# Operand sums spread over the tiles, S3 weights in their own buffer, and a new order of loads, scans and attention around the Strassen products of a hybrid decoder block

## The chip, the cores and the metric

The kernel runs on one core of one Trainium2 chip. The metric is device time in microseconds (us) of one execution, lower is better. The profile was taken in one execution of its own.

## The reference

One decoder block for 2048 tokens of width 1024 in float32, cut here to what matters:

```python
h = rms_norm(x, norm_g)
proj = h @ w_in                              # 1024 x 8704: the largest product
u_ssm, z_ssm, q, k, v, z_attn, q_mem, z_mem, gate_logits = split(proj)
y = gelu(s5_ssm(u_ssm, ...))                 # 48 groups of 16 channels, state 64
y = y * sigmoid(y @ w_glu + b_glu)
o_ssm = y * silu(z_ssm)
o_attn = dilated_window_attention(q, k, v) * silu(z_attn)    # 12 heads of 64, 3 dilations
o_mem = softmax(q_mem @ k_mem.T) @ v_mem * silu(z_mem)       # 4 heads, 256 keys from mem
gates = sigmoid(gate_logits + b_gate)
merged = gates[0] * (o_ssm @ w_br_ssm) + gates[1] * (o_attn @ w_br_attn) + gates[2] * (o_mem @ w_br_mem)
out = rms_norm(x + merged @ w_out, final_norm_g)
```

## The kernel before

**Split products.** Every float32 product is made of three matmuls. Each operand is split into a high part, rounded for the matmul, and a low part, the rest: `three_pass` (line 137) issues high·high (line 138), high·low (139) and low·high (140). The high part comes from a copy on ScalarE (ACT), the low part from a subtraction on VectorE (DVE).

**Stages.** From 0 to about 92 us the kernel normalises x, makes the keys and values of `mem` and the first two tiles of the projection. To about 698 us follow the projection's tiles n = 2 to 27, each 128 columns of `w_in` for all 2048 tokens, in four chunks c of 512 tokens. ACT copies a chunk out of its bank (line 1425), GpSimd (POOL) stores the tile (`store_tile`). Beside them DVE and ACT make the tables of the S5 scan in 12 units u of two tiles each, from n = 4 (`table_slot`; `combine`, line 1908, is one of their steps on DVE, `cs` on ACT at 1503 the cosines), whose small matrices PE multiplies at line 2703. SP stores them (`keep_inputs`, `keep_cosines`).

**The products of Strassen's form (Winograd's variant).** The other 40 tiles of the projection are done in 40 blocks b, each two tiles by half of the tokens (NBK = 40), with seven products instead of eight: A11, S2, S4, A12, S3, A22, S1 in that order, where the S4 of a block comes at step 2 of the next one. The S factors are sums of weights: S1 = A21 + A22 (`sum_s1`, line 2239), S3 = A11 − A21, S2 = S1 − A11, S4 = A12 − S2, each on DVE; then `factor_hi` on ACT and `factor_lo` on DVE (2263) split a factor into one of five places. S3 is written over A21, S2 over A11. SP loads the raw weights (`load_a11` and so on, line 1012). The other side are sums of h, the operands, made during the tiles by POOL: `make_operands(q)` makes the seven sums for one of 8 parts q in eight instructions (first line 1187) in the buffer `hx` and stores them; the next part waits for that store. Parts 0 to 3 belong to the first half of the tokens used, 4 to 7 to the second. The operands are loaded at the entry (line 1038), and exchanged for those of the other half of the tokens after blocks 7 and 27 (`SWAPS`): SP loads 1 MB per operand, `operand_hi` on ACT and `operand_lo` on DVE (2269) split it. DVE adds the products of a block up (`add_u2` 2281, `add_u3` 2288, `add_c12`, `add_c22` 2306); ACT finishes blocks (`finish`, 1463).

**The order beside the products.** Each engine runs the same loop over steps v = 7·row + at, with its own work of a step written out by hand, and all queues are in order. A block has eight side slots j (j = 8b to 8b + 7; s = j // 2), in which other work lies: the S5 scans in 24 pairs of groups (pair p at s = 4 + 2p; matmul 2725), then the bias tables, dilated attention in 40 batches (beat = j − 128 before the change; end at beat A_END = 102; matmuls 2809), attention into `mem` from M0 = A_END + 4 (queries at 2851), its weighing from C_FIRST, then the loads of y, GELU and the first split of y for the GLU product. From about 1794 us to 1893 runs the GLU product, then the branches' projections, the merge, the output projection and the norm.

Of the kernel before, what the change touches and what calls it, by code (L numbers as in the profile page):

```python
# [30 lines left out]
P = 128  # L31
# [31 lines left out]
def build_program(nc, x_t, mem_t, x_n, mem_n, norm_g, mem_norm_g, final_g, w_in, w_kv, b_gate, ssm_par, ssm_d, w_glu, b_glu,  # L63
                  w_br, w_out, rel_bias, buckets, ident_c, anti_c, sign_c, steps_c, powers_c, y_out):
    ctx = ExitStack()
    with ctx:
# [145 lines left out]
        def numbered(table, before=()):  # L212

            n = {x: k + 1 for k, x in enumerate(before)}
            for v in range(N_STEPS + NPR):
                row, at = divmod(v, NPR)
                for what, later in table.get(at, ()):
                    if 0 <= row + later < NBK:
# [6 lines left out]
                         5: ((A22, 1),), 6: ((S2, 1),)}, ((A11, 0), (A22, 0), (S2, 0)))  # L225
        SUM = numbered({4: ((S1, 1), (S3, 1)), 5: ((S2, 1),), 6: ((S4, 1),)},
# [74 lines left out]
        S0, S_BIAS = 4, 8  # L301
        grp_loaded = [sem(f"grp_loaded{i}") for i in range(R)]
# [49 lines left out]
        M0 = A_END + 4  # L352
# [6 lines left out]
        C_EXP, C_FIRST, N_WEIGH = M0 + 8, M0 + 20, NH // 2 * NQ  # L359
# [184 lines left out]
        w_s1, w_s4 = (keep1[:, k, :].rearrange("p (k m) -> p k m", k=4) for k in range(2))  # L544
        FACTOR_RAW = (w_a11, w_a11, w_s4, w_a12, w_a21, w_a22, w_s1)
# [4 lines left out]

        def product_bank(b, i):
            return bank(b, ("c11", "u", "c22", "c11", "u", "c21", "c22")[i])
# [37 lines left out]
        N_FIRST = len(FIRST)  # L590
        WARM = (22, 6)
# [117 lines left out]
        with nc.Block() as block:  # L709
            @block.sync  # L710
            def _(sp):
# [79 lines left out]
                def table_slot(n, c):  # L791
# [9 lines left out]
                    if 0 <= u - 1 < NU and w == 1:  # L801
                        keep_inputs(u - 1)
                        keep_cosines(u - 1, 1)
# [130 lines left out]
                def memory_beat(beat):  # L934
                    if beat == M0 - 1:
                        sp.wait_ge(o_mm, NT_B)
                        for i in range(2):
                            sp.wait_ge(stored[i], 16 * (N_Z // 2))
                            load_queries(i)
                        sp.wait_ge(st_mm, 1)  # L940
                        sp.wait_ge(o_raw, 16 * (NH // 2))
# [7 lines left out]
                        sp.wait_ge(st_out, 1)  # L949
                        for w in range(2):  # L950
                            sp.dma_start(st_d[w, 0:P, :], ptr[:, w, 0:P]).then_inc(st_kept, 16)
                            sp.dma_start(st_d[w, P:NH * NBLK, :], ptr[0:NH * NBLK - P, w, P:2 * P]).then_inc(
                                st_kept, 16)
                        load_stats()
# [17 lines left out]
                def attention_over():  # L972
                    for i in range(2):
                        sp.wait_ge(om_kept[i], 16 * MH)
                    for i in range(RW):
                        sp.wait_ge(oa_kept[i], 16 * N_WEIGH // RW)
# [2204 lines left out]
```

## Time and profile before

| what | value |
|---|---|
| time, median of 3 runs | 2433.62 us (2430.3 to 2434.28) |
| the profiled execution: its own time | 2435.78 us |
| the profiled execution: its span | 2434.0 us |
| mean granted TensorE clock | 0.992 of full speed |
| TensorE (PE) busy | 2351.8 us, 97% |
| VectorE (DVE) busy | 1812.0 us, 74% |
| ScalarE (ACT) busy | 790.5 us, 32% |
| GpSimd (POOL) busy | 288.9 us, 12% |

The span runs from the first to the last instruction that the profiler records; an execution's own time is somewhat longer. Busy times are sums of an engine's instructions. A wait is idle time of an engine, put down to the instruction or transfer that released it last. The granted clock is the share of full speed that TensorE had in a stretch.

### The profile page before, as it was taken

The numbers are of one execution on the slowest core, as the hardware profiler recorded it, in microseconds if no ns is written. First come the engines' busy times: TensorE is split into PE (matmuls) and PEld (weight loads), VectorE is DVE, ScalarE is ACT, GpSimd is POOL, SyncE is SP. The second block draws the span as 40 slices with busy tenths as digits, with TensorE's granted clock in tenths as the row PEclk, the third lists the DMA queues.
The fourth block names the chain that finished last, engine by engine and source line by source line (L and its number), as shares of the span: only waits on it lengthen the run. The fifth ranks groups of instructions, "written<-read, shape, count | busy, mean of one in ns | idle before, by whom it ended". The sixth has DMA issues, their size and how long they took to land. (4 is left out here: it accounts for less than half of the span.)

```text
span 2434.0 us, 32928 instructions
## 1 busy us (share of the span) xinstructions
PE 2351.8 (97%) x12142; PEld 1899.3 (78%) x12142; DVE 1812.0 (74%) x3232; ACT 790.5 (32%) x1633; POOL 288.9 (12%) x400
## 2 busy tenths in 40 slices
PE   9999999999989998999999998999899999999998
PEld 8888887777867776777777786888778888888887
DVE  7366778888767778866788786778575778787775
ACT  5222122212242334335555565444452111110201
POOL 0130022232001111110000000111100000000000
PEclk9999999999999999999999999999999999999999
DMA  8242334444455566553433474589844865758571
GB/s 330 100 144 87 100 122 148 141 137 143 133 182 177 175 230 222 191 164 132 155 129 127 149 290 130 183 271 287 280 163 149 290 178 175 234 181 244 158 234 57
DMA packets 194627, 433.27 MB, mean 178 GB/s; under 512 B 29343, under 2 KB 74499, under 8 KB 184996
## 3 DMA queue, kind: packets, MB, share of 16 engines
q1 hardware_dynamic: 154852, 274.89, 35.7%
q0 software_dynamic: 38576, 154.19, 18.4%
q8 instruction: 97, 1.59, 0.3%
q10 hardware_dynamic: 1040, 2.10, 0.2%
q14 instruction: 62, 0.51, 0.1%
HBM read 284.95 MB, written 146.11 MB: 177 GB/s over the span
## 5 line engine op out<-in xcount | busy, mean ns | idle before, releaser
L138 PE MATMUL bank<-h_hi,w_hi 128*128 128x512 f32 (+1 forms) x2336 | 936.1, 401 | 45.3 <-DVE h_lo L2269 12.2
L140 PE MATMUL bank<-h_hi,w_lo 128*128 128x512 f32 (+1 forms) x2336 | 911.3, 390 | 0.0
L139 PE MATMUL bank<-h_lo,w_hi 128*128 128x512 f32 (+1 forms) x2336 | 910.4, 390 | 0.0
L138 PEld LDWEIGHTS bank<-h_hi,w_hi 128*128 128x128 f32 x2336 | 441.2, 189 | 155.2 <-issue 42.4
L140 PEld LDWEIGHTS bank<-h_hi,w_lo 128*128 128x128 f32 x2336 | 440.7, 189 | 93.8
L139 PEld LDWEIGHTS bank<-h_lo,w_hi 128*128 128x128 f32 x2336 | 441.6, 189 | 87.9 <-issue 1.2
L138 PE MATMUL bank<-h_hi 128*128 128x512 f32 (+1 forms) x688 | 265.7, 386 | 9.1 <-ACT keep L1463 3.2
L140 PE MATMUL bank<-h_hi,h_lo 128*128 128x512 f32 (+1 forms) x688 | 258.5, 376 | 0.0
L139 PE MATMUL bank<-h_lo,h_hi 128*128 128x512 f32 (+1 forms) x688 | 258.3, 375 | 0.0
L138 PEld LDWEIGHTS bank<-h_hi 128*128 128x128 f32 x688 | 129.7, 189 | 38.8 <-issue 13.0
L1436 ACT ACTIVATE w_hi<-w_raw 128x512 fp32r<-128x512 f32 x159 | 99.7, 627 | 160.2 <-PE bank L140 137.3
L139 PEld LDWEIGHTS bank<-h_lo,h_hi 128*128 128x128 f32 x688 | 129.9, 189 | 23.8 <-issue 1.4
L140 PEld LDWEIGHTS bank<-h_hi,h_lo 128*128 128x128 f32 x688 | 129.8, 189 | 23.8
L2263 DVE TENSOR_TENSOR w_lo<-w_raw,w_hi 128x512 fp32r<-128x512 f32 x159 | 108.3, 681 | 37.0 <-ACT w_hi L1436 36.9
L1755 ACT ACTIVATE h_hi<-tb 128x512 fp32r<-128x512 f32 x32 | 20.2, 632 | 342.7 <-DVE tb L2500 342.7
L1425 ACT ACTIVATE ev<-bank 128x512 f32<-128x512 f32 x112 | 64.2, 591 | 203.3 <-PE bank L140 200.3
L130 DVE CAST w_hi<-w_raw 128x1024 fp32r<-128x1024 f32 (+1 forms) x81 | 56.0, 691 | 78.0 <-PE bank L140 59.6
L1524 ACT ACTIVATE tsc<-tsc,stat 128x256 f32<-128x256 f32 (+1 forms) x192 | 88.4, 466 | 61.4 <-DVE stat L2128 61.4
L132 DVE TENSOR_TENSOR w_lo<-w_raw,w_hi 128x1024 fp32r<-128x1024 f32 (+1 forms) x81 | 98.6, 1218 | 2.8
L1503 ACT ACTIVATE cs<-tx 128x256 f32<-128x256 f32 x48 | 20.0, 417 | 247.1 <-DVE tx L1902 133.8
L2125 DVE SCALAR_TENSOR_TENSOR tsc<-bank,bias 128x512 f32<-128x512 f32 x80 | 54.8, 685 | 51.9 <-PE bank L2787 42.9
L2490 DVE SCALAR_TENSOR_TENSOR gt<-gt,bank 128x512 f32<-128x512 f32 x96 | 61.0, 681 | 36.0 <-PE bank L140 22.2
(302 smaller groups left out, 2980.4 us busy)
## 6 DMA issues: line engine op xcount, KB each, us to landing
w_raw<-w_in SPq DMA_DIRECT2D x160, 256.0 KB, 4.0
gt<-proj_d POOLq DMA_DIRECT2D x32, 768.0 KB, 7.8
proj_d<-ev POOLq DMA_DIRECT2D x22, 1024.0 KB, 5.0
proj_d<-ev POOLq DMA_DIRECT2D x81, 256.0 KB, 3.9
proj_d<-keep POOLq DMA_DIRECT2D x79, 256.0 KB, 3.9
lo_raw<-hx_d SPq DMA_DIRECT2D x18, 1024.0 KB, 7.8
w_raw<-w_br SPq DMA_DIRECT2D x32, 512.0 KB, 4.4
wx_raw<-w_br SPq DMA_DIRECT2D x32, 512.0 KB, 4.2
```

Of the source, the lines that this page charges most:

```text
L130: nc.vector.tensor_copy(hi, raw[:, s, 0:kt, :]).then_inc(w_hi_done, 1)
L132: nc.vector.tensor_tensor(lo, raw[:, s, 0:kt, :], hi.bitcast(F32), ALU.subtract).then_inc(w_split[s], 1)
L138: nc.tensor.matmul(out, ah, bh, start=(start and n == 0), stop=False, skip_group_check=onto)
L139: nc.tensor.matmul(out, ah, bl, start=False, stop=False, skip_group_check=onto)
L140: last = nc.tensor.matmul(out, al, bh, start=False, stop=(stop and n == len(pairs) - 1), skip_group_check=onto)
L1425: nc.scalar.activation(dst, src, ACT.Copy).then_inc(evac_done, 1)
L1436: nc.scalar.activation(factor(b, i)[0], FACTOR_RAW[i], ACT.Copy).then_inc(wh_done[0], 1)
L1524: nc.scalar.activation(e, e, ACT.Exp, bias=stat[:, 0, at:at + 1], scale=-1.0, accum_out=stat[:, 1, at:at + 1]).then_inc(e_done, 1)
L1755: nc.scalar.activation(m_tile(h_hi, n), tb[:, :], ACT.Copy, scale=0.5).then_inc(m_hi_done, 1)
L2125: nc.vector.scalar_tensor_tensor(out, sc, -SCALE, bi, ALU.mult, ALU.add).then_inc(s_biased, 1)
L2263: nc.vector.tensor_tensor(lo, FACTOR_RAW[i], hi.bitcast(F32), ALU.subtract).then_inc(wl_done[0], 1)
L2490: nc.vector.scalar_tensor_tensor(gates[:, 2 - b, :], gates[:, 2 - b, :], 1.0, psum[3 * (n % 2) + b][:, :], ALU.add, ALU.mult).then_inc(b_g ...
```

## The change

- **Operand sums.** `make_operands(q, quarter)` makes a fourth of a part: quarters 0 and 1 two sums each of h, 2 and 3 two further steps each, the last with the store. Parts 0 and 1 are made whole at n = 2, 2 and 3 at n = 3 (before: 0 and 1 at n = 3); parts 4 to 7 in quarters at n = 6 to 21 (before, parts 2 to 7 whole, at n = 13, 15, 17, 19, 21, 23 for q = 2 to 7).
- **S3** is written to a buffer of its own (`keep1[:, 2]`). A21 is then loaded two blocks ahead, at step 4. The four sums lie at steps 2, 3, 4, 5 (before 4, 4, 5, 6), and S2 is split at step 5, before A22 at 6.
- **Entry.** In the last tile SP stores tables ahead of the operand loads; A11 and A22 of block 0 are split a chunk earlier, the last unit's cosines lie behind the sums on DVE, the first scan's loads come a slot earlier, and the second block's A21 and A22 are loaded ahead of the loop.
- **Scans.** From pair 13 on they come three slots s (six j) later. **Attention** starts at beat = j − 124; attention into `mem` keeps its place (M0 = A_END + 8), its first queries are loaded at A_END + 3, and the store of the statistics is put ahead of their reload and the gates. C_EXP and C_FIRST move by the same four slots.
- **The end.** y is loaded in single pieces at slots 300, 302, 306 and GELU runs at 306, 310, 316 (before: three loads together at slot 304; GELU at 306, 308, 310). The last block's S4 goes to a bank of its own, with one more addition on DVE, and the first low part of y is split behind the factors of steps 5 and 6.

The diff, cut to its core. The tables and names:

```diff
-                         5: ((A22, 1),), 6: ((S2, 1),)}, ((A11, 0), (A22, 0), (S2, 0)))
-        SUM = numbered({4: ((S1, 1), (S3, 1)), 5: ((S2, 1),), 6: ((S4, 1),)},
+                         5: ((S2, 1),), 6: ((A22, 1),)}, ((A11, 0), (A22, 0), (S2, 0)))
+        SUM = numbered({2: ((S1, 1),), 3: ((S3, 1),), 4: ((S2, 1),), 5: ((S4, 1),)},
...
+        P_PAUSE, PAUSE = 13, 3
+        def pair_slot(p):
+            return S0 + 2 * p + (PAUSE if p >= P_PAUSE else 0)
...
-        M0 = A_END + 4
+        B0 = 124
+        M0 = A_END + 8
...
-        FACTOR_RAW = (w_a11, w_a11, w_s4, w_a12, w_a21, w_a22, w_s1)
+        FACTOR_RAW = (w_a11, w_a11, w_s4, w_a12, w_s3, w_a22, w_s1)
...
+        def last_product(b, i):
+            return (b, i) == (NBK - 1, S4)
         def product_bank(b, i):
+            if last_product(b, i):
+                return bank(b, "u")
...
+        LOAD_Y, GELU = (300, 302, 306), (306, 310, 316)
```

On SP:

```diff
-                    if beat == M0 - 1:
+                    if beat == A_END + 3:
                         sp.wait_ge(o_mm, NT_B)
                         for i in range(2):
...
                             load_queries(i)
+                    if beat == M0 - 2:
                         sp.wait_ge(st_mm, 1)
+                        sp.wait_ge(st_out, 1)
+                        for w in range(2):
+                            sp.dma_start(st_d[w, 0:P, :], ptr[:, w, 0:P]).then_inc(st_kept, 16)
...
+                    if beat == M0:
+                        load_stats()
...
                 def load_a21(b):
                     if b:
-                        sp.wait_ge(*count(wl_done, PREP[S3, b - 1]))
+                        sp.wait_ge(*count(ws_done, SUM[S3, b - 1]))
...
-                        if (n, c) == (NT - 2, 0):
-                            attention_over()
-                            for i in range(3):
-                                sp.dma_start(y_raw[:, i, :, :], y_chunk(i)).then_inc(yr_loaded[i], 16)
+                        if j in LOAD_Y:
+                            load_y(LOAD_Y.index(j))
+                        if j == LOAD_Y[2] + 4:
                             load_first(0)
                             load_first(4)
                         table_slot(n, c)
-                        if s == S0 - 1:
+                        if s == S0 - 2:
                             tables_over()
                             load_pair_of_groups(0)
                             load_pair_of_groups(1)
...
+                        table_slot(n, c)
                         if n == N_Z - 1 and c:
...
                             for i in ((S2, S3), (A22,), (S1,))[c - 1]:
                                 load_operand(0, i)
-                        table_slot(n, c)
+                            if c == 2:
+                                keep_cosines(NU - 1, 1)
+                load_a21(1)
                 load_a22(1)
+                keep_inputs(NU - 1)
...
-                    if at == 2 and row + 1 < NBK:
-                        load_a21(row + 1)
+                    if at == 4 and row + 2 < NBK:
+                        load_a21(row + 2)
```

On POOL:

```diff
-                    for q in range(8):
-                        if n == (3, 3, 13, 15, 17, 19, 21, 23)[q]:
-                            make_operands(q)
+                    if n < 4:
+                        for q in (2 * n - 4, 2 * n - 3):
+                            for quarter in range(4):
+                                make_operands(q, quarter)
+                    elif 6 <= n < 22:
+                        make_operands(4 + (n - 6) // 4, (n - 6) % 4)
```

On ACT:

```diff
-                        if n == N_Z - 1 and c == 2:
+                        if n == N_Z - 1 and c == 1:
                             factor_hi(0, A11)
                             factor_hi(0, A22)
...
                     if at == 5:
+                        factor_hi(row + 1, S2)
+                    if at == 6:
                         factor_hi(row + 1, A22)
-                    if at == 6:
-                        factor_hi(row + 1, S2)
```

On DVE:

```diff
-                    nc.vector.tensor_tensor(w_a21, w_a11, w_a21, ALU.subtract).then_inc(ws_done[0], 1)
+                    nc.vector.tensor_tensor(w_s3, w_a11, w_a21, ALU.subtract).then_inc(ws_done[0], 1)
...
+                        if at == 3:
+                            sum_s3(row + 1)
                         if at == 4:
-                            sum_s1(row + 1)
-                            sum_s3(row + 1)
+                            sum_s2(row + 1)
                         if at == 5:
-                            sum_s2(row + 1)
-                        if at == 6:
                             sum_s4(row + 1)
-                    if (row, at) == (NBK - 1, 6):
-                        y_low(0)
+                    if (row, at) == (NBK, 0):
+                        dve.wait_ge(*count(add_done, ADD["c22", NBK - 1]))
+                        nc.vector.tensor_tensor(u2(NBK - 1), bank(NBK - 1, "c22"), u2(NBK - 1),
+                                                ALU.add).then_inc(p1_done[0], 1)
...
                     if at == 2:
                         factor_lo(row, S1)
+                        if row + 1 < NBK:
+                            sum_s1(row + 1)
...
+                    if row == NBK - 1 and at in (5, 6):
+                        y_low(0, (at - 5,))
```

## Rows read from the trace of the kernel before

**Rows 1.** The page: the span, and each engine's busy time, share and instructions.

```profile
span 2434.0 us, 32928 instructions
PE 2351.8 (97%) x12142; PEld 1899.3 (78%) x12142; DVE 1812.0 (74%) x3232; ACT 790.5 (32%) x1633; POOL 288.9 (12%) x400
```

**Rows 2.** Waits of PE: line, what it waited for: us, times, longest.

```profile
PE bank L138 <- DVE h_lo L2269: 13.7, 6, 5.0
PE bank L138 <- DVE w_lo L2263: 10.6, 11, 1.7
PE bank L2703 <- DVE ca L1908: 8.6, 5, 1.7
PE bank L138 <- DVE ev L2288: 8.5, 1, 8.5
PE bank L138 <- ACT ev L1425: 7.8, 8, 1.7
PE bank L2851 <- DMA qm<-proj_d: 3.6, 1, 3.6
PE bank L138 <- ACT keep L1463: 3.2, 1, 3.2
PE bank L138 <- DVE ev L2281: 2.7, 1, 2.7
PE bank L2725 <- DMA mats<-mats_d: 2.2, 1, 2.2
PE bank L138 <- DVE h_lo L2263: 2.1, 1, 2.1
PE bank L138 <- DVE ev L2306: 2.0, 1, 2.0
```

**Rows 3.** Windows: us, busy of PE, PEld, DVE, ACT, POOL, clock, DMA share, GB/s.

```profile
698.00:1794.00 1096.00, 1043.14 (x6046) 817.76 (x6045) 824.07 (x1432) 507.06 (x1147) 139.83 (x248) 0.99 0.58 191
...
900.00:950.00 50.00, 42.94 (x189) 31.35 (x188) 43.20 (x66) 23.12 (x36) 8.04 (x14) 0.93 0.80 274
...
1450.00:1500.00 50.00, 40.12 (x272) 31.43 (x270) 39.68 (x54) 33.53 (x81) 3.77 (x7) 0.93 0.54 198
...
1750.00:1800.00 50.00, 36.27 (x143) 28.72 (x142) 23.66 (x28) 27.62 (x30) 4.32 (x8) 0.86 0.55 205
```

**Rows 4.** Timeline about 395 us, POOL and DVE: start, us, instruction.

```profile
394.87 5.01 POOL L1187 TENSOR_TENSOR hx<-h_hi,h_lo 128x512 f32<-128x512 f32 x4
394.67 5.83 DVE L1908 TENSOR_TENSOR ca<-ca,tmp 128x576 f32<-128x576 f32 x1
```

**Rows 5.** Timeline of 90 to 165 us; in brackets idle time before and its releaser.

```profile
92.34 0.57 POOL L1176 DMA_DIRECT2D proj_d<-ev  x1 [4.74 <-ACT ev L1425]
114.72 5.41 POOL L1187 TENSOR_TENSOR hx<-h_hi,h_lo 128x512 f32<-128x512 f32 x4
132.78 1.28 POOL L1187 TENSOR_TENSOR hx<-h_hi,h_lo 128x512 f32<-128x512 f32 x1 [5.98 <-DMA hx_d<-hx]
159.19 0.76 DVE L1908 TENSOR_TENSOR ca<-ca,tmp 128x576 f32<-128x576 f32 x1
162.05 0.41 PE L2703 MATMUL bank<-ca,bb 128*16 128x128 f32 x8
```

**Rows 6.** Timeline of the last tile, SP's queue and ACT.

```profile
687.57 5.23 SPq L779 DMA_DIRECT2D mats_d<-kpad  x8
695.31 0.42 ACT L1503 ACTIVATE cs<-tx 128x256 f32<-128x256 f32 x1 [7.50 <-DMA cs_d<-cs]
```

**Rows 7.** Waits of DVE, columns as in rows 2: the sum S1.

```profile
DVE keep L2239 <- DMA w_raw<-w_in: 56.6, 15, 18.8
```

**Rows 8.** The page, DMA issues: transfer, queue, count, KB each, median us to landing.

```profile
w_raw<-w_in SPq DMA_DIRECT2D x160, 256.0 KB, 4.0
```

**Rows 9.** Timeline of SP's queue in the last block of the products.

```profile
1740.83 6.35 SPq L1047 DMA_DIRECT2D y_raw<-ys_d  x3
...
1753.76 1.16 SPq L1012 DMA_DIRECT2D w_raw<-w_in  x1
```

More of the change, by code:

```diff
@@ L301, in build_program, with pair_at @@
         S0, S_BIAS = 4, 8
+        P_PAUSE, PAUSE = 13, 3
+        def pair_slot(p):
+            return S0 + 2 * p + (PAUSE if p >= P_PAUSE else 0)
+        def pair_at(s, lag):
+            at = [p for p in range(NPAIR) if pair_slot(p) == s - lag]
+            return at[0] if at else None
         grp_loaded = [sem(f"grp_loaded{i}") for i in range(R)]
@@ L800, in table_slot @@
                                 load_par(u + 1)
-                    if 0 <= u - 1 < NU and w == 1:
+                    if 0 <= u - 1 < NU - 1 and w == 1:
                         keep_inputs(u - 1)
@@ L970, in y_chunk, with load_y @@
                     return ys_d[:, :, CW * c:CW * (c + 1)].rearrange("k p t -> p k t")
[L972 to L976, printed above, removed]
+                def load_y(c):
+                    if c == 0:
+                        for i in range(RW):
+                            sp.wait_ge(oa_kept[i], 16 * N_WEIGH // RW)
+                    if c == 2:
+                        for i in range(2):
+                            sp.wait_ge(om_kept[i], 16 * MH)
+                    sp.dma_start(y_raw[:, c, :, :], y_chunk(c)).then_inc(yr_loaded[c], 16)
                 def load_glu(n):
@@ L2224, in side_beat, with y_low @@
                         weigh(w)
-                def y_low(c):
+                def y_low(c, parts=None):
                     for part, ks in enumerate(y_parts(c)):
+                        if parts is not None and part not in parts:
+                            continue
                         dve.wait_ge(ys_hi_done, 2 * c + part + 1)
@@ L2311, in add_c12 @@
                         dve.wait_ge(*count(add_done, ADD["u2", b]))
-                        nc.vector.tensor_tensor(u2(b), bank(b, "c22"), u2(b), ALU.add).then_inc(add_done[0], 1)
+                        if b == NBK - 1:
+                            dve.wait_ge(*count(p1_done, NBK + 1))
+                        nc.vector.tensor_tensor(u2(b), product_bank(b, S4), u2(b), ALU.add).then_inc(add_done[0], 1)
                 def split_glu(s, done):
@@ L2928, in side_slot @@
                     s, half = divmod(j, 2)
-                    if half == 0 and (s - S0) % 2 == 0 and 0 <= s - S0 <= G:
-                        if s - S0 < G:
-                            pair_inputs((s - S0) // 2)
-                        if s - S0:
-                            pair_outputs((s - S0) // 2 - 1)
-                    side_beat(j - 8 * (N_GATE - N_Z))
+                    if half == 0:
+                        if pair_at(s, 0) is not None:
+                            pair_inputs(pair_at(s, 0))
+                        if pair_at(s, 2) is not None:
+                            pair_outputs(pair_at(s, 2))
+                    side_beat(j - B0)
                     if half == 1:
@@ L2969, in _ @@
                     for k in range(4):
+                        onto = i in (A12, S3, S4) and not last_product(b, i)
                         mm = three_pass(product_bank(b, i), [((a_hi[:, k, :], a_lo[:, k, :]), (b_hi[:, k, :], b_lo[:, k, :]))],
-                                        start=(k == 0 and i not in (A12, S3, S4)), stop=(k == 3),
-                                        onto=(i in (A12, S3, S4)))
+                                        start=(k == 0 and not onto), stop=(k == 3), onto=onto)
                         if k == 3:
```

119 lines of the change are left out of this document (63 added, 56 removed).

## The prediction, made before the changed kernel was run

> **What bounds the kernel now.** The page's first block comes first [rows 1]: TensorE (PE) is busy 2351.8 of 2434.0 us, the next engine, VectorE (DVE), 1812.0. The change leaves the number of matmuls as it is, so what it can take away is the 82 us in which PE is idle and the time PE loses at a lowered clock. Next comes the list of PE's waits [rows 2]: eleven of its lines name work that the diff touches, and add up to 65.0 us (13.7 + 10.6 + 8.6 + 8.5 + 7.8 + 3.6 + 3.2 + 2.7 + 2.2 + 2.1 + 2.0). The rest of the idle time (start, attention's own turns, the end) belongs to lines that it doesn't move. Last the windows [rows 3]: in the three stretches of 50 us that hold the longest of these waits the granted clock is 0.93, 0.93 and 0.86, while it is 0.99 over the whole loop of products. That loop's 1096.00 us give 27.4 for a block of seven products, 3.9 for a product and 3.4 for one of its eight side slots. Each of the waits is then read in its own stage: which engine was late, and what stood ahead in that engine's queue.
>
> **A. Operand sums spread.** POOL makes the seven sums of h in eight rounds of 8 instructions. While its four adds run back to back (5.01 us), one add of DVE that began 0.2 us ahead of them takes 5.83 us [rows 4]; the same instruction takes 0.76 with POOL idle [rows 5]. DVE loses 5.1 us per burst, and PE's five waits at line 2703 are the second half of that. The change runs four of the rounds in four pieces of 2 instructions, one per tile: a burst is 2.5 us (half of 5.01), DVE loses about 2.6, and the five waits were 1.7 us each, so 8.6 go. The line-1425 wait (7.8, eight times) is PE waiting for its bank, whose reader ScalarE (ACT) stood behind late DVE tables: 6.1 of it falls into these tiles and goes with the same cause, 1.7 is the longest, at the entry (part B). Returned: 14.7.
> The price: rounds q0 to q3 now run back to back from the end of the store at 92.34 + 0.57 = 92.9, where before there were two, at 114.72 and 132.78 [rows 5]. A round takes 132.78 − 114.72 = 18.06 us, because the next one waits for the landing of its store (the 5.98). So the rounds start near 93, 111, 129 and 147, and the fourth lies on DVE's first matrices. DVE loses 5.1 for its first four instructions and 3/4 of that, 3.8, for the three that follow, since the eighth falls behind; 8.9 together, of which I give back 2, about half of the second burst, as the earlier rounds end sooner. These matrices end at 159.19 + 0.76 = 159.95 and PE takes them at 162.05 [rows 5], a cover of 2.1. A new wait of 8.9 − 2 − 2.1 = 4.8, bounds 0 (the matrices have slack that I overlook) and 9. **Net of A: 14.7 − 4.8 = 9.9.**
> The Trainium skill speaks against this reading ("SBUF — State Buffer", section "Who interferes with whom"): of DVE and GpSimd, the one that issues first has the shared port pair for its whole instruction and the other blocks; issue order decides, not the shape. By that the add of DVE, which began first, would not have been held; the row shows 5.83 us for it. By the rule the sum would be without A's 14.7.
>
> **B. Entry to the products.** SP (the sync engine's queue) issues three operand loads of 1 MB and only then the stores of the last table unit (687.57, 5.23 for eight of them); the cosine on ACT at 695.31 has stood 7.50 us for them [rows 6]. Behind it lie four waits of PE: 1.7 (line 1425), 2.1 (h_lo of line 2263), 2.7 (line 2281) and 2.2 (matrices of the first scan), together 8.7 [rows 2]. The change issues table stores first, loads the second block's weights ahead of the loop, and takes A11 and A22 a unit earlier. SP's three loads are the same, only later; what they hold up then is the operand of the second product, which was loaded several us ahead. The stretch saved, up to 7.50, is more than the largest wait. I leave 0.5 for the first scan's loads. **8.2.**
>
> **C. S3 in its own buffer.** S3 was summed into A21's buffer, so A21 of the next block could be loaded only when S3 had been split, and DVE waited 56.6 us in 15 places at line 2239 for that load [rows 7]. Its splits stand behind the sum in the same queue: PE's eleven waits of at most 1.7 at w_lo [rows 2]. Now A21 is loaded two blocks ahead and the four sums stand one per product. The sums are the same instructions; the new buffer costs no time. What hides the reordering S2 before A22: DVE was 43.2 of 50 us busy in the densest window [rows 3], so there is room, thinly. Cover that shrinks: A22's load waits for A22's low part, now one product later, with three products (11.7 us) left before the sum that needs it; such loads land in 4.0 us at the median [rows 8]. I leave 1; the ends are none and, if only the eleven waits change their place, all 10.6. **9.6.**
>
> **D. Exchanges.** Operands change places after blocks 7 and 27. At the first DVE has 43.20 of 50 us of work [rows 3], scans among it, and the fresh operand's low part waits its turn: 13.7 us in six waits, the longest 5.0 at the second exchange [rows 2]. The change leaves three scan slots empty there, and has attention start four slots sooner (13.7 us), so that it is over before the second. The price: scans of pairs 13 and up end six slots later, so that between their end and attention's first loads there are ten slots less. By the tables of slots the last pair is stored at slot 112, attention's first loads are issued at 116 and attention begins at 124, which still leaves 13.7 us ahead of the loads. I leave 1.5 for ACT, which stays behind its stores at the second. **12.2**, bounds 6 and 13.7.
>
> **E. Memory attention.** One wait for queries, 3.6 [rows 2], is for a load issued just ahead of its use; it is now issued five slots ahead. SP's queue has the statistics' stores and reload behind it; only weighing waits for those, later. **3.6.**
>
> **F. The end of the products.** SP issued three loads of y in one go (1740.83, 6.35 us of issue), and behind them the last A21 load, at 1753.76 [rows 9]; DVE's longest wait for weights, 18.8, is this one [rows 7]. On PE it becomes 3.2 + 8.5 + 2.0 = 13.7 (lines 1463, 2288, 2306) [rows 2]. Now the loads come one at a time at slots 300, 302 and 306, the last S4 takes a bank of its own at the cost of one more add on DVE (0.76 by the nearest row, the add in [rows 5]), and y's low parts are cut in two. I leave 1. **12.7.**
>
> **Clock.** (1 − clock) × 50 in the three windows is 3.5 + 3.5 + 7.0 = 14.0 [rows 3]. Part of the lowered stretch lies in PE's idle time, where it costs nothing, so 14.0 is the upper end and 0 the lower. I take half, 7.0, less 0.5 for the waits that remain and 1.1 for A's new one (14.0 lost beside 30.7 us of idle time in the windows is 0.46 per us; half of that by 4.8): **5.4.**
>
> **Sum.** 9.9 + 8.2 + 9.6 + 12.2 + 3.6 + 12.7 + 5.4 = 61.6. Removing eleven waits lets PE run up to others that they covered; for these I take 4: 57.6. The profiled execution, 2435.78 us, lies 2.2 above the median of 2433.62. So 2378 for its like, and 2433.6 − 57.6 = **2376** for the median.
>
> **Rivals.**
> R1, the waits come back halved: DVE's queue is in order and 86% full in the exchange window; what moved out of one slot is late in the next. Half of C, D, F and the clock (20) and the 4 of the cover doubled: 57.6 − 24 = 34, so 2400. For: DVE's share there; against: most of the eleven waits are caused by a load, not by DVE's work.
> R2, A fails: DVE's loss isn't POOL's burst, or pieces of 2 hold it as long as four. Then 14.7 stay and the new wait comes too: 2376 + 14.7 = 2391. Against: 5.83 beside 0.76. By the rule of the Trainium skill named in A it would end here.
> R3, the end isn't cured: the y loads and the last weights still meet in SP's queue, or PE now waits for the last add. 12.7 + about 3 of clock: 2392. For: seven transfers still fall into the last block.
> R4, slower: A22's load, now behind A22's low part, lands too late for S1's sum in every block. If DMA contention makes it miss by x, PE loses x in 38 blocks; above 57.6 / 38 = 1.5 us each it eats the gain. It needs landings of more than 11.7 + 1.5 us against 4.0 [rows 8]. At 3 us each: 2376 + 114 = 2490.
> That the change doesn't do what it says (the pause misses the exchange by a slot) would leave D's 12.2: inside the range.
>
> **How the numbers follow.** Chances: the forecast, 2366 to 2388, 0.60; R1 0.17; R2 0.08; R3 0.10; R4 and the like 0.05. Bounds: A's new wait 0 to 9 (±4.5), the clock 0 to 14 (±7), D 6 to 13.7. These together make some ±10; towards R1 to R3 the range goes to 2402, downwards to 2360 (the clock in full, no new wait). A measurement of this kernel can tell about 0.2%, 5 us, from no change. Faster by over that: all but R4 and a part of R1, 0.92; within 0.04; slower 0.04.
>
> **What would show it.** A: no PE wait at line 2703 between 400 and 600, DVE's held adds near 3.2 instead of 5.83, and one wait of about 5 near 162; none there, or one of 9, corrects this term. B: ACT's cosine no longer idle 7.50 before it. C: the 56.6 at line 2239 gone, and no w_lo among PE's waits; S1's sum waiting for A22's load would be R4. D: no h_lo waits at line 2269, though a new line for a scan or for attention would be R1. F: no 18.8, PE not idle over 2 us between 1700 and 1750. Clock: the windows of those places at 0.98 or more. Wrong above all if PE's idle total falls by less than 40 us.

## The result, and the profile of the changed kernel

The changed kernel takes 2411.07 us (median of 4 runs, 2407.48 to 2413.54) beside 2433.95 before: a ratio of 0.9908, 95% interval 0.9889 to 0.9927. It is faster, but by 22.9 us where 57.6 were forecast, and 9 us outside the stated range.

The page of the changed kernel, its first lines (answering rows 1), and below them the waits of PE (rows 2; line, what it waited for: us, times, longest):

```profile
span 2411.7 us, 32933 instructions
PE 2351.3 (97%) x12142; PEld 1903.1 (79%) x12142; DVE 1805.6 (75%) x3233; ACT 795.5 (33%) x1637; POOL 288.9 (12%) x400
```

```profile
PE bank L138 <- DVE h_lo L2305: 13.5, 6, 4.3
PE bank L138 <- DVE ev L2317: 10.5, 5, 4.3
PE bank L2749 <- DVE ca L1942: 5.6, 1, 5.6
PE bank L2855 <- ACT tsc L1558: 5.6, 1, 5.6
PE bank L138 <- ACT keep L1497: 4.5, 1, 4.5
PE bank L2838 <- DMA va<-v_d: 3.9, 1, 3.9
...
PE bank L138 <- DVE ev L2350: 0.5, 1, 0.5
```

Lines have moved: 2305 is the operands' low part (before 2269), 2317 `add_u2` (2281), 2749 the table matrices (2703), 2855 attention's transposes (2809), 1497 ACT's finish of a block (1463), 2350 `add_c12`. In the experiments built on the changed kernel the numbers differ by up to three where lines were added or taken out above; those built on the kernel before have its numbers. Idle time of PE is 2411.7 − 2351.3 = 60.4 us, where it was 82.2; its busy time is 2351.3, where it was 2351.8. So 21.8 of the 22.3 gained in the span are idle time, and the lowered clock gave nothing back. That is not the chance of one execution: the mean granted clock of the four of the changed kernel was 0.989 to 0.991, that of the kernel before, in all its runs here, 0.988 to 0.992. Windows of the changed kernel (columns as in rows 3):

```profile
150.00:200.00 50.00, 44.38 (x193) 35.89 (x192) 41.54 (x84) 10.53 (x22) 18.83 (x16) 0.93 0.48 159
...
900.00:950.00 50.00, 42.83 (x192) 31.46 (x191) 41.96 (x71) 16.14 (x28) 6.11 (x11) 0.93 0.51 154
...
1400.00:1450.00 50.00, 41.76 (x294) 33.32 (x293) 33.67 (x50) 34.01 (x95) 3.78 (x7) 0.90 0.70 263
...
1700.00:1750.00 50.00, 43.35 (x188) 35.23 (x187) 26.59 (x49) 23.75 (x40) 6.47 (x12) 0.93 0.73 258
```

Set beside the sum of the prediction:

| term | forecast | read from PE's waits |
|---|---|---|
| A, operand sums | 14.7 − 4.8 | 14.7 − 5.6 |
| B, entry | 8.2 | 8.7 |
| C, weights | 9.6 | 10.6 |
| D, exchanges | 12.2 | 13.7 − 13.5 = 0.2 |
| E, queries | 3.6 | 3.6 |
| F, end | 12.7 | 13.7 − 4.5 = 9.2 |
| new waits | −4 | −10.5 − 5.6 − 3.9 − 0.5 = −20.5 |
| clock | 5.4 | 0.5 |
| sum | 57.6 | 21.4 of the 22.3 |

Four of the terms (A, B, C, E) came as worked out, to a microsecond, and F came 3.5 short. Three failed: D gave nothing, the clock gave nothing, and the new waits are five times what was set aside.

Where the new waits come from is read in the queues. The waits of DVE for transfers, first for the kernel before (its 56.6 us at S1 are rows 7), then for the changed one (the weighing, the product with the factors `fb`, is line 2193 before and 2224 after; S1 is 2239 and 2272, S3 after the change 2280):

```profile
DVE oa L2193 <- DMA fb<-f_d: 4.2, 5, 1.8
```

```profile
DVE oa L2224 <- DMA fb<-f_d: 39.0, 7, 8.8
DVE keep L2280 <- DMA w_raw<-w_in: 19.1, 5, 6.4
...
DVE keep L2272 <- DMA w_raw<-w_in: 3.2, 1, 3.2
```

And SP's own waits for split factors ahead of weight loads, before and after:

```profile
SPq L1012 <- DVE w_lo L2263: 298.9, 92, 8.2
```

```profile
SPq L1034 <- DVE w_lo L2299: 357.7, 52, 22.1
```

The longest of them, 22.1 us, shows the mechanism. In the timelines of SP, DVE and PE of the changed kernel (start, us, instruction; in brackets idle time before and its releaser):

```profile
1380.62 0.33 SPq L1034 DMA_DIRECT2D w_raw<-w_in  x1
1403.13 0.33 SPq L1034 DMA_DIRECT2D w_raw<-w_in  x1
...
1404.46 0.43 SPq L894 DMA_DIRECT2D va<-v_d  x1
```

```profile
1402.42 0.68 DVE L2299 TENSOR_TENSOR w_lo<-w_raw,w_hi 128x512 fp32r<-128x512 f32 x1
```

```profile
1411.72 1.88 PE L2838 MATMUL bank<-ka,qa 64*128 64x128 f32 x16 [3.88 <-DMA va<-v_d]
```

SP issues nothing from 1380.95 until DVE's split of A22 ends at 1403.10; 0.03 us later it issues the load of A22, and then, behind it, the keys and values of attention that PE waits for. The same at the weighing, on DVE and PE; `add_u2` comes behind the weighing on DVE:

```profile
1651.76 0.69 DVE L2224 TENSOR_TENSOR oa<-oa,fb 128x512 f32<-128x512 f32 x1 [8.82 <-DMA fb<-f_d]
...
1653.70 0.69 DVE L2317 TENSOR_TENSOR ev<-bank,keep 128x512 f32<-128x512 f32 x1
```

```profile
1654.44 0.80 PE L138 MATMUL bank<-h_hi,w_hi 128*128 128x512 f32 x1 [4.26 <-DVE ev L2317]
```

### The profile page after: what moved, and what is told of

Read it like the earlier page. It is cut to its first block and busy times, and to the rows that moved or that the text cites. A ratio compares the mean times of both kernels' runs of the same rounds, so it can differ in the third digit from the quotient of the medians.

```text
span 2411.7 us, 32933 instructions
## 1 busy us (share of the span) xinstructions
PE 2351.3 (97%) x12142; PEld 1903.1 (79%) x12142; DVE 1805.6 (75%) x3233; ACT 795.5 (33%) x1637; POOL 288.9 (12%) x400
## 5 line engine op out<-in xcount | busy, mean ns | idle before, releaser
L138 PE MATMUL bank<-h_hi,w_hi 128*128 128x512 f32 (+1 forms) x2320 | 928.9, 400 | 21.9 <-DVE h_lo L2305 13.5
L138 PE MATMUL bank<-h_hi 128*128 128x512 f32 (+1 forms) x704 | 271.4, 386 | 12.2 <-DVE ev L2317 5.3
L140 PE MATMUL bank<-h_hi,h_lo 128*128 128x512 f32 (+1 forms) x704 | 265.0, 376 | 0.0
L139 PE MATMUL bank<-h_lo,h_hi 128*128 128x512 f32 (+1 forms) x704 | 264.8, 376 | 0.0
L1470 ACT ACTIVATE w_hi<-w_raw 128x512 fp32r<-128x512 f32 x129 | 80.9, 629 | 179.1 <-PE bank L140 112.5
L130 DVE CAST w_hi<-w_raw 128x1024 fp32r<-128x1024 f32 (+1 forms) x81 | 62.7, 774 | 101.8 <-PE bank L140 84.1
L2299 DVE TENSOR_TENSOR w_lo<-w_raw,w_hi 128x512 fp32r<-128x512 f32 x129 | 88.2, 684 | 9.3 <-ACT w_hi L1470 9.2
L2299 DVE TENSOR_TENSOR w_lo<-keep,w_hi 128x512 fp32r<-128x512 f32 x91 | 62.4, 686 | 36.2 <-ACT w_hi L1470 36.1
L2536 DVE SCALAR_TENSOR_TENSOR gt<-gt,bank 128x512 f32<-128x512 f32 x96 | 61.0, 682 | 37.8 <-PE bank L140 23.1
```

The source lines that it names most:

```text
L130: nc.vector.tensor_copy(hi, raw[:, s, 0:kt, :]).then_inc(w_hi_done, 1)
L138: nc.tensor.matmul(out, ah, bh, start=(start and n == 0), stop=False, skip_group_check=onto)
L139: nc.tensor.matmul(out, ah, bl, start=False, stop=False, skip_group_check=onto)
L140: last = nc.tensor.matmul(out, al, bh, start=False, stop=(stop and n == len(pairs) - 1), skip_group_check=onto)
L1470: nc.scalar.activation(factor(b, i)[0], FACTOR_RAW[i], ACT.Copy).then_inc(wh_done[0], 1)
L2299: nc.vector.tensor_tensor(lo, FACTOR_RAW[i], hi.bitcast(F32), ALU.subtract).then_inc(wl_done[0], 1)
```

## Experiments on SP's queue and the order of the splits

Theory T1: the change splits A22 at step 6 instead of 5; SP waits for that split at its own step 6, ahead of all that it has to issue there, so every load behind comes late. Rival T2: the weighing, moved four slots ahead, or the traffic makes them late.

The runs come from several sessions, in which the kernel before had medians of 2433.36 to 2435.5 us; a difference between kernels of different sessions is uncertain by about 2 us.

**A22's load a step later**, in the changed kernel:

```diff
                     if at == 0 and row + 1 < NBK:
                         load_a11(row + 1)
+                        if row:
+                            load_a22(row + 1)
-                    if at == 6 and row + 2 < NBK:
-                        load_a22(row + 2)
```

> The changed kernel with one edit: SP issues the load of A22 for the block after next not at step 6 ahead of that step's slots, but a step later, behind the load of A11. Theory T1: in the changed kernel A22's low part comes at the end of step 6 on DVE, SP waits for it there with everything else that it has to issue queued behind (its waits at the weight loads for w_lo are up to 22.1 us long, 8.2 before the change), so the loads for weighing and for attention come late; PE's five waits at add_u2 (10.5 us), the one for va (3.9) and perhaps the one behind ACT's o_d store (5.6) come from it. Then these go, about 14 to 20 us with the clock, so 2391 to 2397. Rival T2: the weighing moved ahead by four slots, or traffic on the DMA engines, makes these loads late; then nothing changes, 2408 to 2413.

Measured: 2386.46 us (2384.65 to 2387.49), 24.6 less than the changed kernel; 0.9800 of before, 0.9784 to 0.9817. PE's waits, and SP's longest group:

```profile
PE bank L138 <- DVE h_lo L2305: 15.9, 9, 4.3
PE bank L2855 <- ACT tsc L1558: 6.2, 2, 5.5
PE bank L2749 <- DVE ca L1942: 5.6, 1, 5.6
```

```profile
SPq L1034 <- DVE w_lo L2299: 208.7, 70, 8.4
```

```profile
DVE oa L2224 <- DMA fb<-f_d: 1.8, 3, 0.9
```

`add_u2`, `va` and the finish at the end (10.5 + 3.9 + 4.5 = 18.9) are gone, SP's longest wait for a split factor there is 8.4 again, and DVE's wait for `fb` falls from 39.0 to 1.8. The gain is larger than expected since the finish at the end hung on the same load, and PE's busy time fell too, to 2341.8, by 9.5. The idle total fell by 16.5, not by 18.9, since the waits for operands and for `tsc` rose by 3.0. The wait behind ACT's `tsc` stays: it is not SP's.

**The weighing back at slot 254**, in the changed kernel:

```diff
-        C_EXP, C_FIRST, N_WEIGH = M0 + 6, M0 + 16, NH // 2 * NQ
+        C_EXP, C_FIRST, N_WEIGH = M0 + 8, M0 + 20, NH // 2 * NQ
```

> The changed kernel with the weighing of the attention's heads back at slot 254 (C_EXP and C_FIRST four slots later), where it was before the change. Rival T2 (the earlier weighing makes its loads late): the five waits at add_u2 (10.5 us) go, 2398 or less. Theory T1 (SP held at A22's load): the waits at add_u2 stay near 10 us in total, four slots later, 2408 to 2414, or a few us more, since the weighing then ends at slot 300, where the loads of y wait for it.

Measured: 2414.41 us. C_FIRST goes back by four slots here and C_EXP by two, which is also what the change had moved them by. The waits at `add_u2` are 10.4 us, as in the changed kernel. T2 falls as far as the place of the weighing goes.

**The order of the splits alone**, in the kernel before (the same exchange of lines on ACT and on DVE, and in the table):

```diff
                     if at == 5:
-                        factor_lo(row + 1, A22)
+                        factor_lo(row + 1, S2)
                     if at == 6:
-                        factor_lo(row + 1, S2)
+                        factor_lo(row + 1, A22)
```

> The kernel before with one edit of the change alone: S2 is split at step 5 and A22 at step 6 (order of ACT, DVE and of the table), everything else as it was. Theory T1: SP waits for A22's low part at the end of step 6 with the loads for attention and weighing behind it, as in the changed kernel, so PE gets waits at add_u2 in the weighing (about 10 us) and at attention's loads (4 or more): 2445 to 2455, SP's waits for w_lo with a longest of over 15 us instead of 8.2. Rival T2 (the earlier weighing or the traffic is the cause): within 3 us of 2434.

Measured: 2442.47 us beside 2433.36, a ratio of 1.0045 (1.0030 to 1.0060): slower by 9.1, as T1 says, less than expected. The waits of PE, DVE and SP tell why it is less:

```profile
PE bank L138 <- DVE ev L2281: 12.8, 6, 3.5
...
PE bank L138 <- DVE w_lo L2263: 1.0, 1, 1.0
```

```profile
DVE keep L2239 <- DMA w_raw<-w_in: 53.6, 16, 19.1
DVE oa L2193 <- DMA fb<-f_d: 36.8, 8, 8.3
```

```profile
SPq L1012 <- DVE w_lo L2263: 386.5, 74, 14.9
```

The order puts in 10 us at `add_u2` (12.8 less the 2.7 of the entry) and takes out 9.6 of the 10.6 at `w_lo`. SP's longest wait is 14.9, just under the 15 expected, and no wait for `va` came. In the profiled execution PE's idle time is 84.9 us, 2.7 more than before, and its busy time 2355.5, 3.7 more: the waits put in are up to 3.5 us long, those taken out at most 1.7. With the weighing and the loads of A21 where they were before the change, `fb` is late all the same, so T2 isn't needed. And the order takes the waits at `w_lo` out while DVE still waits 53.6 us for A21: the cause that step C gave for the waits at `w_lo` is not needed for them to go. Two more runs separate the order from the S3 buffer.

**The changed kernel with the old order** (the edit above the other way round; S3 buffer, early A21 and spread sums stay):

> The changed kernel with A22 split at step 5 and S2 at step 6 again, as before the change, so that of part C the S3 buffer, the load of A21 two blocks ahead and the spread sums stay. If the order of the two splits alone took away PE's waits for w_lo (theory from f1_before_swap, where 10.6 us became 1.0 while DVE still waited 53.6 us for A21), they come back here, to between 5 and 10 us, and the waits at add_u2, va and the copy at the end (18.9) go, since SP is no longer held: 2395 to 2402. If the S3 buffer took them away (the prediction's step C), they stay away: 2386 to 2390, as in e1_a22_next.

Measured: 2392.49 us (2389.89 to 2393.34), between both expectations. The waits at `add_u2`, `va` and the finish at the end are gone. PE's waits for split factors are 2.8 + 1.5 (the second row is the same split into a place that lies in the tile `h_lo`):

```profile
PE bank L138 <- DVE w_lo L2299: 2.8, 5, 1.0
...
PE bank L138 <- DVE h_lo L2299: 1.5, 2, 0.8
```

**The kernel before with the new order and A22's load a step later:**

> The kernel before with two edits: S2 split at step 5 and A22 at 6 (as in f1_before_swap), and A22's load a step later behind A11's (as in e1_a22_next). If the order is what cures the waits for w_lo, and SP's place is what the order costs: no w_lo and no add_u2 among PE's waits over 3 us, 10.6 us and some clock less than before, 2418 to 2423. If the S3 buffer is needed, the sum S1 at step 4 now waits longer for A22 and A21 and PE with it: 2430 or more.

Measured: 2419.57 us, a ratio of 0.9934 (0.9918 to 0.9951). No `w_lo` over 1 us and no `add_u2` but the entry's, though DVE's wait for A21 stands:

```profile
DVE keep L2239 <- DMA w_raw<-w_in: 52.9, 16, 18.2
```

So either edit takes the waits at `w_lo` down, the order to 1.0, the buffer with early loads and spread sums to 4.3. Of the 56.6 us of DVE in rows 7, 18.8 are the one wait in the last block, which did cost PE (here 18.2, with 11.5 us of PE's waits at the end); the other 37.8 cost PE next to nothing, for 34.7 of them stand here too, beside 1.0 us at `w_lo`.

## Experiments on the exchanges

**A pause of six:**

```diff
-        P_PAUSE, PAUSE = 13, 3
+        P_PAUSE, PAUSE = 13, 6
-                        if j == B0 - 8:
+                        if j == B0 - 4:
                             groups_over()
```

> The changed kernel with the pause of the scans six slots s long instead of three, and attention's first loads four slots j later so that they still follow the last scan. Theory: the fresh operands are split on DVE at the steps of slots j = 60 to 71, while the pause frees j = 58 to 65 only, so that the scans of pairs 13 and 14 (j = 66 to 71) stand ahead of two operands and PE waits 4.2 and 2.9 us at about 905 and 926 us. With six they lie behind the exchange: 7.1 us of waits and about 2 of clock go, 2402. Rival: the operands are late because of ACT or of SP's loads; then the waits stay where they are and the time is 2408 to 2413.

Measured: 2401.85 us, the expected time, in part by luck. Where the changed kernel waits 4.22 and 2.93 at the first exchange, the timeline of PE has 2.4 us in two, so 4.8 of the 7.1 went:

```profile
896.94 0.47 PE L138 MATMUL bank<-h_hi,w_hi 128*128 128x512 f32 x1 [1.29 <-DVE h_lo L2305]
901.01 0.47 PE L138 MATMUL bank<-h_hi,w_hi 128*128 128x512 f32 x1 [1.08 <-DVE h_lo L2305]
```

The rest of the gain is PE's busy time, 3.8 less where about 2 had been counted, and waits that were not in the sum: those at `add_u2` are 8.3 instead of 10.5, the one for the finish at the end 3.2 instead of 4.5. Why these two fell no run shows.

The changed kernel there, DVE and PE: scan pair 13 (lines 2094 to 2102) starts inside the exchange and the operand's split is behind it.

```profile
898.49 1.29 DVE L2094 TENSOR_TENSOR tv<-bank,csb 128x512 f32<-128x512 f32 x2
...
900.49 1.27 DVE L2102 TENSOR_TENSOR_SCAN zv<-m8b,wv 128x256 f32<-128x256 f32 x2
901.67 0.67 DVE L2299 TENSOR_TENSOR h_lo<-w_raw,h_hi 128x512 fp32r<-128x512 f32 x1
902.26 2.35 DVE L2305 TENSOR_TENSOR h_lo<-lo_raw,h_hi 128x1024 fp32r<-128x1024 f32 x2
```

```profile
904.76 0.77 PE L138 MATMUL bank<-h_hi,w_hi 128*128 128x512 f32 x1 [4.22 <-DVE h_lo L2305]
```

**No pause, attention six slots earlier:**

```diff
-        P_PAUSE, PAUSE = 13, 3
+        P_PAUSE, PAUSE = 13, 0
-        B0 = 124
-        M0 = A_END + 8
+        B0 = 118
+        M0 = A_END + 14
```

> The changed kernel without the pause of the scans and with attention started six slots earlier still (beat = j - 118; attention into mem keeps its place). Theory: attention ends at slot 226 in the changed kernel while the second exchange runs over slots 220 to 231, so four slots were too few; started at 118 it ends at 220, and PE's waits for fresh operands at about 1440 to 1463 (6.3 us) go. At the first exchange the waits come back to what they were before the change, 7.1 in four, which is what the changed kernel has in two: the three slots of pause gave nothing. So about 2403. Rival: ACT's copies of the operands or SP's loads make the second exchange late; then the 6.3 stay and the time is 2408 to 2413, or more if the first exchange gets worse.

Measured: 2394.58 us, better than the expected 2403. At the second exchange 1.31 + 1.07 = 2.4 remain of 6.3, and the first has 6.4 in three, less than with the pause of three. Gone as well, and not expected, are attention's waits behind `tsc` (5.6) and `va` (3.9); a wait of 4.0 for ACT at 1068 is new, and those at `add_u2` are 12.5. The one behind `tsc` is, in the changed kernel, ACT standing 9.96 us for a store that POOL issued behind the store of a block:

```profile
1372.58 0.54 POOL L1255 DMA_DIRECT2D proj_d<-ev  x1 [8.69 <-ACT ev L1497]
1373.11 0.54 POOL L1265 DMA_DIRECT2D o_d<-ev  x1
```

```profile
1383.29 1.02 ACT L1580 ACTIVATE ev<-bank 128x512 f32<-128x512 f32 x1 [9.96 <-DMA o_d<-ev]
```

That attention's place within the block decides this is argued from these rows; no run moved attention alone. (With the pause of six and attention as in the changed kernel, 5.1 of the 5.6 stay.)

**The operands' low parts ahead of the side slots of their step:**

```diff
+                    for swap in SWAPS:
+                        done = product_at(v - 5) if v >= 5 else None
+                        if done is not None and done[0] == swap:
+                            operand_lo(stage_of(swap) + 1, done[1])
                     if product_at(v) is not None:
                         for j in slots_in(v):
                             side_slot(j)
```

(The same four lines behind the slots are taken out.)

> The changed kernel with the operands' low parts on DVE ahead of the side slots of their step instead of behind them; pause and attention as in the changed kernel. Theory: at both exchanges PE waits because scans (first) and attention (second) stand ahead of the split in DVE's queue, not because of ACT or of the loads. Then most of the 13.5 us goes, to 2 or 3, with 2 to 4 of clock: 2396 to 2400. Rival: SP's loads of 1 MB or ACT's copies are late; then DVE waits for them at the new place, the side work is late too, and the time is 2408 or more.

Measured: 2405.42 us, 5.6 less than the changed kernel and 5 to 9 short of the expectation. The waits for operands fall from 13.5 to 9.3, those behind `tsc` rise from 5.6 to 9.4. At the first exchange waits of 1.36 and 3.82 are left of 4.22 and 2.93, where the pause of six leaves 2.4 in all. The order within a step is the smaller part there; that the scans as a whole put DVE behind PE is argued from this.

## Experiments on the operand sums

**Three parts at the start instead of four**, the other five in quarters over tiles 4 to 23:

```diff
-                        for q in (2 * n - 4, 2 * n - 3):
+                        for q in ((0, 1), (2,))[n - 2]:
...
-                    elif 6 <= n < 22:
-                        make_operands(4 + (n - 6) // 4, (n - 6) % 4)
+                    elif 4 <= n < 24:
+                        make_operands(3 + (n - 4) // 4, (n - 4) % 4)
```

> The changed kernel with three instead of four parts of the operand sums made whole at the start (parts 0 and 1 at tile n = 2, part 2 at n = 3) and the other five in quarters over the tiles 4 to 23. Theory: the fourth whole part lies on DVE's first table matrices and makes PE's wait of 5.6 us at 167.6 us and the lowered clock behind it (0.93 in 150 to 200, 3.5 us at most); without it both go, 2402 to 2406, and no wait for tables appears in the tiles. Rival: the wait has another cause (DVE's own tables began late); then it stays.

Measured: 2406.28 us, at the upper end. The wait at the first matrices falls from 5.6 to 1.7; the quarter at tile 4 still lies on them (POOL from 157.00 for 2.54 us, an add of DVE from 157.09 for 3.08). With the quarters over tiles 6 to 25, in the runs below, it is gone.

**The old places**, `n == (3, 3, 13, 15, 17, 19, 21, 23)[q]`, all four quarters at once:

> The changed kernel with the operand sums where they were before the change: parts 0 and 1 whole at tile n = 3, parts 2 to 7 whole at n = 13 to 23. Theory A of the prediction: DVE is held up by POOL's bursts of four adds, so PE's waits for the tables (8.6 us at the table matrices, 6.1 for ACT's copies) come back, and the wait of 5.6 at 167 us and its lowered clock (about 2) go: 2411 + 14.7 - 7.6 = 2418, all of A's net. Rival: the adds of POOL don't hold DVE, what DVE lost before the change had another cause that the change removed too; then only the 5.6 and the 2 go, 2403.

Measured: 2420.02 us (2414.73 to 2424.96), 9 more than the changed kernel, as expected. The waits are back, 12.3 of the 14.7, and the new one is gone; these are of the profiled execution, at 2414.73 the fastest of the six:

```profile
PE bank L2747 <- DVE ca L1940: 6.9, 4, 1.7
PE bank L138 <- ACT ev L1457: 5.4, 7, 1.4
```

## The edits together

**A22's load, three parts with the rest over tiles 6 to 25, operands first:**

> The changed kernel with three edits together: A22's load a step later in SP's queue (as in e1_a22_next), three parts of the operand sums at the start and five in quarters over the tiles 6 to 25, and the operands' low parts ahead of the side slots (as in e7_op_first). If the three causes are apart, the gains add: 24.6 by the run of e1_a22_next, 5 to 7 for the sums, 12 to 15 for the exchanges, so 2366 to 2370. If they overlap (one wait covers another), 2375 to 2386.

Measured: 2373.96 us. The single gains were 24.6, 4.8 (with the quarters two tiles earlier) and 5.6, 35.0 together; the three in one gave 37.1, 4 to 8 short of the expectation, which had counted more for the exchanges than the single run gave. It lies only 1 us under the range for an overlap (2375 to 2386), but the single gains as measured add up within the noise, so the causes are apart.

**A22's load, a pause of six, the sums:**

> The changed kernel with three edits: A22's load a step later (e1_a22_next), the pause of six (e2_pause6), three operand parts at the start and five over the tiles 6 to 25. If the causes are apart: 2411 - 24.6 - 9 - 6 = 2371. At the first exchange two waits of about 1.2 us remain, at the second 4 to 6 us, and one of about 5.5 behind ACT's o_d store.

Measured: 2372.47 us, and the waits are those expected: 1.29 and 1.06 at the first exchange, 1.28 and 4.30 at the second, 5.62 behind the store of o_d.

**Operands first, no pause, attention at slot 118:**

> The kernel of c2_a22_first_even with no pause and attention started at slot 118 (as in e3_attn6). Theory: the waits at the second exchange (4.6 us in c2_a22_first_even) fall to about 1.5, those behind ACT's o_d store (8.3) go, and the first exchange has 5 to 6 as there: 2374 - 3 - 8 = 2363, some 2 less with the clock. Rival: what attention leaves at the second exchange is filled by attention into mem, or its own loads come late: 2370 or more.

Measured: 2361.44 us (2361.09 to 2362.54), 0.9704 of before (0.9689 to 0.9718), the fastest: 72 us less than before. Its span is 2359.3 us, with PE busy for 2336.7. PE's longest waits:

```profile
PE bank L138 <- DVE h_lo L2308: 7.1, 4, 2.5
...
PE bank L138 <- DVE ev L2353: 1.7, 1, 1.7
```

**The same with the operands behind the slots:**

> As c3_attn6_first, with the operands' low parts behind the side slots as in the changed kernel. Theory: in e7_op_first the other order gave only 5.6 us, because DVE as a whole runs behind PE in the exchange and the order within a step moves the wait by at most one step; so 1 to 4 us slower than c3_attn6_first at the first exchange (6.4 instead of 5 to 6). If the order decides: 6 us slower.

Measured: 2363.88 us, 2.4 more, as expected: the order within a step is worth that much.

## Why the prediction was wrong, and where it was right

The forecast gain was 57.6, and the table finds 21.4. Of the 36.2 that are missing, 16.5 are new waits, 12.0 are D, 4.9 the clock and 3.5 F; the differences of A, B and C come to 0.7 the other way. PE's idle total fell by 21.8, where the prediction had named less than 40 as the sign of being wrong above all.

- **A was right, in mechanism and size.** Rounds started at 92.86, 112.71, 131.94 and 151.06 (forecast 93, 111, 129, 147), the new wait was 5.6 at 167.59 for 4.8, and DVE's add held by a burst of two took 3.15 (forecast 3.2) where one without took 0.69:

```profile
400.51 2.54 POOL L1215 TENSOR_TENSOR hx<-h_hi,h_lo 128x512 f32<-128x512 f32 x2
```

```profile
399.73 0.69 DVE L1920 TENSOR_TENSOR tmp<-pw_sai,bbs 128x512 f32<-128x512 f32 x1
400.46 3.15 DVE L1942 TENSOR_TENSOR ba<-ba,tmp 128x512 f32<-128x512 f32 x1
```

  This add again began ahead of POOL's, by the profile's starts, and was held for the length of the burst. By the rule named in the prediction (the Trainium skill, "SBUF — State Buffer", section "Who interferes with whom": issue order decides who blocks) it would have kept its 0.69; these starts speak against it. The section also says that a DVE instruction with two SBUF inputs contends with a GpSimd instruction that reads SBUF, which the prediction leaves out: a hold as such agrees with it, and it is the order that these starts speak against.

  In the fourth round the loss came in another shape. DVE was at small instructions there, and beside POOL's back-to-back adds each took about the time of one of them:

```profile
151.06 5.05 POOL L1215 TENSOR_TENSOR hx<-h_hi,h_lo 128x512 f32<-128x512 f32 x4 [5.97 <-DMA hx_d<-hx]
```

```profile
152.42 1.21 DVE L1920 TENSOR_TENSOR sm_fr<-sm_t,sm_den 128x4 f32<-128x4 f32 x1
```

```profile
167.59 0.63 PE L2749 MATMUL bank<-ca,bb 128*16 128x128 f32 x8 [5.62 <-DVE ca L1942]
```

  Instructions of the same shapes that were not held took 0.16 to 0.23 there, so the eight held ones between 151.24 and 161.73 cost 8.4 us in all, where 8.9 were forecast, as one burst and three fourths of another. Undoing the edit cost 9.0 by the medians, for a forecast net of 9.9. R2 falls.
- **B and E were right**: no wait of theirs is left.
- **C failed at the step "cover that shrinks".** It saw that A22's load now waits for a split one product later, and priced the load: three products left before S1. That was right (S1 waited 3.2 us in all) and beside the point. What was not asked, though it is the first question for any wait that is moved on an in-order queue, is what SP has queued behind that wait: the loads of the same step for weighing and attention, issued only a few slots ahead of use. With the load moved, 18.9 us of waits and 9.5 us of PE's busy time went. R4 stood at the right instruction with the wrong victim. The other half of C, why the waits at `w_lo` would go, had the right size by luck: C counts the reordering as a price only, and it is the reordering that takes 9.6 of the 10.6 out by itself, while the buffer, the early loads and the spread sums alone leave 4.3.
- **D failed at the step "so that it is over before the second".** The slots were in the prediction's own tables: attention ends at 124 + 102 = 226, and the second exchange's splits lie at slots 220 to 231. The first runs over 60 to 71, and the pause frees 58 to 65. Neither sum was made. That scans and attention hold up the operands was right: the pause of six leaves 2.4 us of waits at the first exchange, attention at 118 leaves 2.4 at the second. The price of 12.2 no run reached; the fastest kernel still has 7.1 of the 13.7, and no run has the pause of six and the earlier attention together.
- **F was right in mechanism, mis-sized by 3.5.** The three loads in one go and the 18.8 are gone. The 4.5 left were SP's delay once more: they went with A22's load.
- **The clock** was taken as a share of the windows before. It goes with the waits that are there after: with 20.5 us of new ones, 0.5 of the 5.4 came back. What was taken out were mostly short waits (the five of A and the eleven of C, none over 1.8 us), while seven of those that are there after are of 3.8 to 5.6 us; the last section has the clock behind either. In the fastest kernel PE's busy time is 2336.7, 15.1 less than before, which is near the upper end of 14.0.
- **New waits: 4 set aside, 20.5 found.** 14.4 of them are SP's (10.5 + 3.9), 5.6 attention's store.
- R1 gave the nearest time, 2400, by a cause (DVE full) that holds for the exchange only. R3 holds in part: the end still met late loads.

## What to carry to other kernels

When an edit moves the event that an in-order queue waits for, price what is queued behind the wait before the waiting instruction itself; a DMA queue's own list of waits, with its longest, shows it at once. When work is moved out of a window, write down both windows in slots first. An engine's long idle time (37.8 us here, outside the last block) need not be the cause of the short waits behind it.

## What the runs showed of the hardware

Idle time on PE cost more than itself in some places, and not in others. From the changed kernel to the one with A22's load a step later PE's idle time fell from 60.4 to 43.9 us and its busy time, for the same 12142 matmuls, from 2351.3 to 2341.8. From the kernel before to the changed one idle time fell by 21.8 and busy time by 0.5 only. From the kernel before to the fastest one the two fell by 59.6 and 15.1.

What differs is which waits went. After the wait of 4.22 us at 904.76 the next twelve matmuls start 0.43 us apart, ahead of it 0.23; the granted clock from 904.76 to 909.90 is 0.50, the lower of the two levels (1.2 of 2.4 GHz). It is 0.50 also in the 4 to 5 us behind the waits of 5.62 (at 167.59) and 4.30 (at 1440.12), and 0.64 behind the 4.26 at 1654.44. It is 1.00 behind the 2.93 at 925.65, and in the kernel before behind the waits of 1.73 at 400.56 and 447.75 for the tables. The length of a wait alone doesn't decide it: behind the 2.47 at 935.88 in the kernel before, the last of four waits for operands there, the clock is 0.61.
